# An attention stage with page copy and merge ahead of the output's low part, and post-norm sums that begin with tile 6

## The reference, cut to what matters

```python
def rmsnorm(x, g):
    y = xf * lax.rsqrt(jnp.mean(xf * xf, axis=-1, keepdims=True) + EPS)
    return (y * g.astype(jnp.float32)).astype(x.dtype)
# after every sub-layer:  x = x + [0.5 *] rmsnorm(y, norm_post)

s = (jnp.einsum('bqhc,bkc->bhqk', ql, kc) + jnp.einsum('bqhr,bkr->bhqk', qp, kpe)) * scale
s = jnp.where(k_pos <= pos, s, -jnp.inf)
p = jax.nn.softmax(s, axis=-1)
return jnp.einsum('bhqk,bkc->bqhc', p, kc)
```

## Time and profile before

| | |
|---|---|
| median of 3 runs | 1488.62 us (1485.42 to 1488.76) |
| profiled execution, device time | 1487.02 us |
| its span, first to last instruction | 1485.4 us |
| PE busy | 1441.1 us (97%) |
| DVE, ACT, POOL busy | 906.4, 744.8, 143.5 us |
| chain that ended last, by engine | PE 87%, DVE 8%, ACT 2%, issue 2% |
| granted PE clock over the span | 0.996 |
| HBM traffic | 149 GB/s over the span |

### The profile page before, as it was taken

One profiled execution on the slowest core, in us unless ns is written; L12 is line 12 of the kernel. 1 busy time (PEld: TensorE's weight loads), 2 busy tenths in 40 slices (PEclk: granted clock), 3 DMA queues, 4 the chain that ended last, 5 costly groups with the idle time before them and its releaser, 6 DMA issues.

```text
span 1485.4 us, 29589 instructions
## 1 busy us (share of the span) xinstructions
PE 1441.1 (97%) x11034; PEld 1367.6 (92%) x11034; DVE 906.4 (61%) x1497; ACT 744.8 (50%) x1200; POOL 143.5 (10%) x211
## 2 busy tenths in 40 slices
PE   8999999999989999999999999999999999999997
PEld 8999998999877989999989999998876688999996
DVE  5655536989867686654376555347655547655534
ACT  5555425678454465554256555345533336555422
POOL 0111000000100001110001111001044300111000
PEclk9999999999999999999999999999999999999999
DMA  5444333333321334344424434444488643434441
GB/s 217 165 146 165 142 141 122 142 143 142 124 109 45 121 114 169 141 143 161 149 98 175 152 141 147 161 145 157 153 282 265 215 164 114 170 141 145 158 149 64
DMA packets 50568, 222.68 MB, mean 150 GB/s; under 512 B 6625, under 2 KB 23138, under 8 KB 28338
## 3 DMA queue, kind: packets, MB, share of 16 engines
q1 hardware_dynamic: 39138, 191.66, 36.1%
q0 software_dynamic: 6192, 24.64, 4.8%
q10 hardware_dynamic: 5152, 5.25, 1.1%
HBM read 214.74 MB, written 6.77 MB: 149 GB/s over the span
## 4 chain that ended last, share of the span: by engine, by line
PE 87%; DVE 8%; ACT 2%; issue 2%; DMA 0%; ACTq 0%; DVEq 0%; SPq 0%
PE psum L247 15%; PE psum L252 15%; PE psum L248 15%; PE psum L340 7%; PE psum L341 7%; PE psum L339 7%; PE psum L2395 2%; PE psum L2353 1%; DVE w_lo L235 1%; ACT w_hi L228 1%; DVE x L404 1%; PE psum L2224 1%; PE psum L1335 1%; DVE y L400 1%; PE psum L1320 1%
## 5 line engine op out<-in xcount | busy, mean ns | idle before, releaser
L235 DVE TENSOR_TENSOR w_lo<-raw,w_hi 128x2048 fp32r<-128x2048 f32 x163 | 378.1, 2319 | 298.1 <-ACT w_hi L228 297.9
L228 ACT ACTIVATE w_hi<-raw 128x2048 fp32r<-128x2048 f32 x158 | 302.8, 1916 | 352.2 <-PE psum L341 208.2
L247 PE MATMUL psum<-h_hi,w_hi 128*128 128x320 f32 x1520 | 451.7, 311 | 1.3 <-ACT w_hi L228 0.6
L248 PE MATMUL psum<-h_lo,w_hi 128*128 128x320 f32 x1520 | 448.8, 309 | 0.0
L247 PEld LDWEIGHTS psum<-h_hi,w_hi 128*128 128x128 f32 x1520 | 285.3, 188 | 2.6 <-ACT w_hi L228 0.9
L248 PEld LDWEIGHTS psum<-h_lo,w_hi 128*128 128x128 f32 x1520 | 285.3, 188 | 0.8
L252 PE MATMUL psum<-h_hi,w_lo 128*128 128x320 f32 x1520 | 254.0, 309 | 0.0
L252 PEld LDWEIGHTS psum<-h_hi,w_lo 128*128 128x128 f32 x1520 | 230.6, 188 | 0.2 <-DVE w_lo L235 0.2
L341 PE MATMUL psum<-hid_hi,w_lo 128*128 (+1 forms) x704 | 217.6, 309 | 0.0
L339 PE MATMUL psum<-hid_hi,w_hi 128*128 (+1 forms) x704 | 217.6, 309 | 0.0
L340 PE MATMUL psum<-hid_lo,w_hi 128*128 (+1 forms) x704 | 217.6, 309 | 0.0
(11 more groups left out here) (429 smaller groups left out, 1940.1 us busy)
## 6 DMA issues: line engine op xcount, KB each, us to landing
raw<-wts SPq DMA_DIRECT2D x164, 1024.0 KB, 4.8
h_plain<-cache_t POOLq DMA_DIRECT2D x44, 160.0 KB, 3.7
h_plain<-cache_t SPq DMA_DIRECT2D x44, 160.0 KB, 3.4
arena<-s POOLq DMA_DIRECT2D x4, 1024.0 KB, 7.0
sgs<-arena POOLq DMA_DIRECT2D x4, 1024.0 KB, 4.4
marena<-cache_t POOLq DMA_DIRECT2D x20, 160.0 KB, 3.3
marena<-cache_t SPq DMA_DIRECT2D x20, 160.0 KB, 3.4
raw<-cache_c SPq DMA_DIRECT2D x16, 128.0 KB, 3.9
```

Source lines behind the costliest of these rows:

```text
L228: act.activation(w_hi[c0 % 2][:, :], raw[c0 % 2][:, :], ACT.Copy).then_inc(hi_ready, 1)
L235: eng.tensor_tensor(w_lo[c0 % 2][:, :], raw[c0 % 2][:, :], w_hi[c0 % 2][:, :].bitcast(F32), ALU.subtract).then_inc(lo_ready, 1)
L247: pe.matmul(outs[n], wtile(w_hi, c0, n * K + k), src_hi(k), start=(k == 0), stop=False)
L248: pe.matmul(outs[n], wtile(w_hi, c0, n * K + k), src_lo(k), start=False, stop=False)
```

## The change

Four orders are changed; no instruction is added or removed, apart from where waits stand. On PE `page_plain_pe(n)` goes ahead of `new_scores_pe`. On ACT `high` goes ahead of `load_first_plain`. On DVE `low` goes behind `copy_plain`, `merge` and `norm`. In `post_stat_pe` the first of the three matmuls is now the square of tile 6, then comes `ssum`, then the square of tile 7.

```diff
@@ post_stat_pe
             pe.wait_ge(y_copied, 3 * s + 1)
+            pe.wait_ge(y_squared, KT * s + NSUM + 2)
+            pe.matmul(o, ones[:, :], sqx[(NSUM + 1) % 4][:, :], start=True, stop=False)
             pe.wait_ge(y_summed, NSUM * (s + 1))
-            pe.matmul(o, ones[:, :], ssum[:, :], start=True, stop=False)
-            for m in range(NSUM + 1, KT):
+            pe.matmul(o, ones[:, :], ssum[:, :], start=False, stop=False)
+            for m in range(NSUM + 2, KT):
@@ attention_pe
                 numerators_pe(pe, n - 1)
+                page_plain_pe(pe, n)
                 if pair_of(n, 3):
                     new_scores_pe(pe, pair_of(n, 3))
-                page_plain_pe(pe, n)
@@ attention_act
+                if finished(n):
+                    high(finished(n) - 1)
                 if n < NUN - 1:
                     load_first_plain(act, n + 1)
-                if finished(n):
-                    high(finished(n) - 1)
@@ attention_dve
-                if finished(n):
-                    low(finished(n) - 1)
                 copy_plain(n)
                 if n > 0:
                     merge(n - 1)
                     if n % NQT == 0:
                         norm(n // NQT - 1)
+                if finished(n):
+                    low(finished(n) - 1)
```

## The result

| | before | after |
|---|---|---|
| median of 6 runs each | 1487.78 us (1485.34 to 1490.33) | 1478.06 us (1477.04 to 1480.14) |
| profiled execution | 1487.02 us | 1480.14 us |
| its span | 1485.4 us | 1478.5 us |
| PE on the chain that ended last | 87% | 90% |
| DVE and ACT on it | 8%, 2% | 7%, 1% |

The ratio is 0.9944 with a 95% interval of 0.9932 to 0.9955. The change takes off 9.7 us by the medians (6.7 to 10.1 by the interval). The forecast was 8.05 us off and 1479.0 us, within 1475.8 to 1483.3.

What follows compares the result with a forecast made beforehand. PE was taken as the bound, so only its waits counted: 5.0 + 0.3 + 2.75 = 8.05 us off 1487.02 us gives 1479.0 us. Range 1476 to 1482, widened to 1475.8 to 1483.3.

Steps and rivals of the forecast that it cites:

- Part 1: Attention, `high` and `low` moved: units 6, 10 and 14 should last as unit 2 does, 5.0 us less.
- Rival 1: Attention: only part of the stall goes, another wait ends last in units 6, 10, 14; 5.6 us, 1481.4 us; chance 0.08.
- Part 2: Attention, `page_plain_pe` moved: page transposes fill PE's idle time ahead of the new scores in unit 1, 0.3 us.
- Part 3: Post-norm sums: tile 6's matmul follows the last dense matmul at once, 0.55 us in each of 5 stages, 2.75 us.
- Rival 2: Post-norm: tile 6's matmul buys nothing, the chain through `ssum` stays as long; 5.3 us in all, 1481.7 us; chance 0.07.
- restart at `ssum`: Post-norm: the end comes 0.59 us earlier, or 0.54 if PE's restart for `ssum` costs a little.
- The sign "about 1.9 us behind the last dense matmul": Post-norm: if right, L363 starts about 1.9 us behind the last dense matmul where it was 2.6.
- The sum: Whole kernel: 5.0 + 0.3 + 2.75 = 8.05 us less, giving 1479.0 us.
- Rival 3: Attention: page transfers become the bound at 253 GB/s, a unit takes 8.29 us; slower, 1490.5 us; chance 0.03.
- issued two units ahead: Attention, argument against transfers as the bound: a page lands 5.5 us behind its issue at most, two units ahead.
- Rival 4: Attention: DVE's page copy holds up POOL's issues until the values wait; 2.0 us of gain lost, 1481.0 us; chance 0.02.

Runs made afterwards that it cites:

- e4: Kernel before with only ACT's order changed, `high` ahead of the page transfers: 1481.29 against 1485.62 us, ratio 0.9970.
- e5: Kernel before with only DVE's order changed, `low` behind page copy, `merge` and `norm`: 1485.40 against 1485.62 us, ratio 0.9991.
- e6: Kernel before with only PE's order changed, page transposes ahead of the new scores: 1486.80 us in one run.
- e7: Kernel after with SP and POOL issuing each unit's pages one unit later: 1488.63 us against 1485.62 for the kernel before, ratio 1.0010.

## Why the prediction was right, point by point

- **Part 1, the stall of attention.** 5.0 us forecast and 5.0 us measured: 1.56, 1.56 and 1.88. The term came from comparing the unit with another unit of the same work instead of from the idle time in brackets. The prediction's lower bound, 2.6 us, took the 0.86 us of unit 6 for all three; the waits of PE for the copy were 2.9 us, with 1.2 in one unit, and those for the prompt unit 0.8 us. Even these 3.7 us stay under the 5.0. Rival 1 rested on the 2.6 and is refuted. What the prediction did not see is that the two moves are not needed together. It argued them as one; e4 shows that ACT's alone gives everything; DVE's alone gives 3.3 us by the trace of e5, which its times leave unconfirmed. In the kernel after, DVE's move is a reserve.
- **Part 2, the page transposes.** 0.3 us forecast with 0.31 as the upper bound, 0.43 measured (e6). The step that failed is the bound: it took the idle time in the row for the whole loss. The idle time in a row counts from the modelled end of the last matmul, and a matmul that follows at once starts ahead of that end: dense matmuls that last 0.31 us start 0.15 us apart.
- **Part 3, the post-norm.** 0.55 us taken per stage, 0.59 to 0.61 measured in all five stages of the profiles with the new order, a little over the bound of 0.59. Stage 5 changed by nothing (1.96 us before, 1.96 or 1.97 after), as forecast. Rival 2 is refuted. The 0.05 us taken off for a restart at `ssum` were not lost in addition, but the wait itself did not vanish: the weight load still waits 0.31 us for `ssum` in stage 0, and stages 0 to 4 end at 2.03 to 2.09 us where stage 5, without that wait, ends at 1.96. The kernel before had such a delay too (from the start of `ssum` to the next 0.62 us, where that of tile 6 now takes 0.54), so the 1.86 us of the prediction already held it. The sign "about 1.9 us behind the last dense matmul" was a slip: the prediction's own sum gives 2.63 - 0.59 = 2.04, and 2.03 was measured.
- **The sum.** 8.05 us forecast, 8.4 us by the traces, 9.7 and 10.1 us by the medians of two comparisons. The mechanism of each part was right. That the measured median, 1478.06 us, came within 1 us of the forecast 1479.0 is partly luck: the forecast started from an execution that had lost 3.2 us to dips, and how many dips the runs after would draw it could not know. The prediction had no term for the clock at all, since the stretches of rows 9 read 1.00, though the mean over the span was 0.996. Whether the clock explains the medians' surplus over 8.4 us is not shown. Both intervals take in the 8.4, and two sets of runs of the kernel before on one chip had medians of 1487.00 and 1485.62 us, 1.4 us apart without any edit.
- **Rival 3, the page transfers.** Rightly held improbable, and for the right reason as to the rate. But the reserve was put too high in one argument, "issued two units ahead". That holds for the transposed pages. The plain pages come last in POOL's queue, and e7 shows that a delay of one unit there costs 10.8 us. The place to look was the queue's order, not the rate or the landing time.
- **Rival 4, POOL and DVE's copy.** Nothing of it: PE was busy for all of 1074 to 1180 us, and a POOL issue that began at 1114.96 us, beside the copy of 1114.53, took the usual 0.54 us. For this copy, which reads PSUM, the trace does not show the lock that the Trainium skill's "SBUF — State Buffer" describes under "SBUF: two separate sides"; that page itself bounds its rule to copies in a two-port mode.

## What to carry to other kernels

When an instruction is late, look at what stands ahead of it in its own engine's queue before moving those that wait for it: here a transfer issue that waits for another engine had been put ahead of two cheap copies, and moving the copies alone gave the whole 5.0 us of that stall. Price a stall by the length of the same work without it, or by starts, and take the idle time in brackets as a lower bound only. Account for the clock in a profile before comparing its span with another. And before calling transfers ahead of time, follow the last one in each queue, not the first.

## What was not expected of the hardware

Three things. Half-clock stretches of PE of about 3 to 4 us came and went between executions of the same kernel, with some 1.6 us lost in each. In the part from L363 of stage 0 to L363 of stage 1 they made the length vary from 276.3 to 281.5 us over 14 profiles (0.6 us of this is the edit's), while the 13 runs of the kernel before in one comparison spread over 6.4 us. One such stretch, behind 1.77 us of idling near 1043 us, came in 6 of 7 profiles of one group and in none of 7 of the other, with an edit between them that does not touch the code there; 14 profiles do not show whether that is more than chance. And a matmul behind an idle gap costs more than the gap in brackets says: 0.43 us by starts for 0.31 us in unit 1, and 0.44 us for 0.23 us in unit 6 of e5.
